# Gate product of an encoder layer: seven half-size block products per pair of token tiles instead of eight, all of h first

## The reference, cut to what matters

```python
mix = concatenate([o_att * silu(g_att), o_lru * silu(g_lru)])        # 512 + 512 channels
h = x + mix @ w_out                                                   # 1024 x 1024
e = (p @ w_ple) * sigmoid(h @ w_pg)                                   # w_ple 256 x 1024, w_pg 1024 x 1024
y = h + rms_norm(e, g_ple)
```

## Time and profile before

| | |
|---|---|
| device time, median of 3 runs | 1025.38 us (1024.9 to 1025.61) |
| span of the profiled execution, first to last instruction | 1022.9 us |
| PE busy | 1001.2 us, 98% |
| DVE, ACT, POOL busy | 657.0, 582.6, 496.6 us |
| matmuls | 5798 |
| granted TensorE clock | 0.999 of full speed |
| transfers | 150.34 MB, 147 GB/s on average |

### The profile page before, as it was taken

One profiled execution on the slowest core, in us unless ns is written; L12 is line 12 of the kernel. 1 busy time (PEld: TensorE's weight loads), 2 busy tenths in 40 slices (PEclk: granted clock), 3 DMA queues, 4 the chain that ended last, 5 costly groups with the idle time before them and its releaser, 6 DMA issues.

```text
span 1022.9 us, 15489 instructions
## 1 busy us (share of the span) xinstructions
PE 1001.2 (98%) x5798; PEld 798.6 (78%) x5798; DVE 657.0 (64%) x1062; ACT 582.6 (57%) x896; POOL 496.6 (49%) x400
## 2 busy tenths in 40 slices
PE   9999999999999999989999999999999999999997
PEld 7867777777788888878777777777788888888886
DVE  5645857592583350579999999999874454535423
ACT  7748485846641231569999999999942221112113
POOL 1163343626557440155676676666676334353421
PEclk9999999999999999999999999999999999999999
DMA  9751543323265527759876577433384223432321
GB/s 344 271 147 37 175 149 104 119 82 134 62 186 171 158 83 207 212 154 232 210 211 174 130 208 174 112 114 125 131 277 139 88 88 109 146 96 88 106 84 42
DMA packets 106329, 150.34 MB, mean 147 GB/s; under 512 B 10248, under 2 KB 69384, under 8 KB 106248
## 3 DMA queue, kind: packets, MB, share of 16 engines
q1 hardware_dynamic: 106112, 149.36, 48.6%
q10 hardware_dynamic: 144, 0.00, 0.0%
HBM read 102.07 MB, written 44.11 MB: 143 GB/s over the span
## 4 chain that ended last, share of the span: by engine, by line
PE 76%; DVE 14%; issue 7%; ACT 1%; POOL 1%; DMA 0%; DVEq 0%; SPq 0%; POOLq 0%; ACTq 0%
DVE E_ L1680 10%; PE b_ps L2008 6%; PE b_ps L2010 6%; PE b_ps L2009 6%; PE b_ps L1870 6%; PE b_ps L1872 5%; PE b_ps L1871 5%; PE g_ps L1872 4%; PE g_ps L1870 4%; PE g_ps L1871 4%; PE o_ps L2065 3%; PE s_ps L2021 3%; PE w_ps L1982 3%; PE h_ps L1870 2%; PE uT_ps L1945 2%
## 5 line engine op out<-in xcount | busy, mean ns | idle before, releaser
L1680 DVE CUSTOM_DVE_ANT_0 E_<-s_ps,bias 128x1024 f32<-128x1024 f32 (+1 forms) x184 | 188.2, 1057 | 10.0 <-PE s_ps L2021 9.8
L1266 ACT ACTIVATE E_<-E_,nmax 128x1024 f32<-128x1024 f32 (+1 forms) x184 | 186.6, 1018 | 13.3 <-DVE nmax L1680 13.3
L995 POOL TENSOR_TENSOR E_<-E_,ratio 128x576 f32<-128x576 f32 (+3 forms) x92 | 84.5, 919 | 92.7 <-DVE E_ L1696 92.7
L998 POOL TENSOR_TENSOR E_<-E_ 128x576 f32<-128x576 f32 (+3 forms) x92 | 103.6, 1126 | 7.2
L1872 PE MATMUL b_ps<-u_hi,wA_lo 128*128 128x512 f32 x256 | 99.8, 390 | 0.0
L2021 PE MATMUL s_ps<-KL,QL 128*128 128x512 f32 x256 | 88.8, 431 | 7.8 <-DVE nmax L1680 7.7
L1281 ACT ACTIVATE WT<-w_ps 128x1024 f32<-128x1024 f32 (+1 forms) x96 | 83.5, 869 | 4.2 <-PE w_ps L1982 3.8
L1982 PE MATMUL w_ps<-ident,E_ 128*128 128x128 f32 x624 | 83.5, 273 | 2.1 <-ACT WT L1281 2.0
L1870 PE MATMUL b_ps<-u_hi,wA_hi 128*128 128x512 f32 x216 | 85.5, 396 | 0.0
L1982 PEld LDWEIGHTS w_ps<-ident,E_ 128*128 128x128 f32 x624 | 72.6, 140 | 15.3 <-issue 6.3
L1871 PE MATMUL b_ps<-u_lo,wA_hi 128*128 128x512 f32 x216 | 84.1, 389 | 0.0
(11 more groups left out here) (265 smaller groups left out, 2420.3 us busy)
## 6 DMA issues: line engine op xcount, KB each, us to landing
QL<-qk_t SPq DMA_DIRECT2D x32, 256.0 KB, 7.3
KL<-qk_t SPq DMA_DIRECT2D x32, 256.0 KB, 8.5
bias<-line_d SPq DMA_DIRECT2D x8, 960.0 KB, 12.1
x_sb<-in_x SPq DMA_DIRECT2D x12, 512.0 KB, 9.0
z_ch<-z_stage SPq DMA_DIRECT2D x24, 256.0 KB, 2.9
qk_t<-qh SPq DMA_DIRECT2D x24, 256.0 KB, 2.3
qk_t<-ql SPq DMA_DIRECT2D x24, 256.0 KB, 2.8
mf<-mix_t SPq DMA_DIRECT2D x24, 256.0 KB, 4.0
```

What stands on the lines that cost most here:

```text
L998: gp.tensor_tensor(one, one, two, ALU.add).then_inc(w_gp, 1)
L1266: act.activation(e, e, ACT.Exp, bias=nmax[:, n % 5, c:c + 1], scale=-1.0, accum_out=sums[:, n % 5, c:c + 1]).then_inc(e_done, 1)
L1680: dve.tensor_tensor_reduce(weights_at(n)[:, c, 0:n_tok], s_ps[:, c, 0:n_tok], b[:, ::-1], -1.0, 3e38, ALU.add, ALU.min, nmax[:, n % 5, c:c ...
```

## The change

The gate product is computed for two token tiles at once, a left operand of 256 x 1,024 cut into four blocks of 128 x 512, A11, A12, A21, A22, against w_pg cut into four of 512 x 512. In place of the eight block products there are seven (Strassen's, in Winograd's form): S1 = A21 + A22, S2 = S1 - A11, S3 = A11 - A21, S4 = A12 - S2 on the left; on the right T1 = W12 - W11, T2 = W22 - T1, T3 = W22 - W12 (in W12's place), T4 = W21 - T2. Each product p1 to p7 is 12 matmuls (`gate_part`) into one of two banks, left_ps and right_ps. Three of the sums of products need a copy on ACT (`copy_sum`) and an addition on DVE (`joined`).

All of h comes first: a stage of its own runs turn_o and mix_product for tiles 1 to 11 and keeps h in four buffers, with tiles 0 to 7 also stored to a new DRAM tensor h_tok and loaded again later. Then six pairs follow, in the order of tiles 8/9, 10/11, 0/1, ... 6/7. The product of the pair's second tile takes part as r = 1, that of its first as r = 0. In the stage of h, from tile 2 on, o's squares are taken on ACT (`square_o`), its root is a reciprocal on DVE (`mean_square`) and a square root on ACT (`root_o`), and the scaling is eight small activations (`scale_o`) in place of one DVE operation. The splits and sums of the gate weights (`gate_weights` on DVE, `gate_high` on ACT, two on POOL) are operations on 2,048 elements, spread over the same stage. In the pairs, sums and splits of the turned h are made for the next pair while this one runs. The last pair is finished in halves of 512.

The sum of the counts: the gate product was 12 x 48 = 576 matmuls of 128x512 and is 6 x 7 x 12 = 504. Transposes of h stay 96, in fours.

```diff
+            def store_h(n):
+                sp.wait_ge(fin["h_done"], n + 1)
+                sp.dma_start(h_tok[n * P:(n + 1) * P, :], h_sb[:, n % 4, :]).then_inc(fin[f"h_out{n % 2}"], 16)
+            def load_h(g, r):
+                t, slot = tile_of(g, r), slot_of(g, r)
+                sp.wait_ge(fin["y_done"], 2 * (g - 2) + 2 - r)
+                sp.wait_ge(fin[f"h_out{t % 2}"], 16 * 4)
+                sp.dma_start(h_sb[:, slot, :], h_tok[t * P:(t + 1) * P, :]).then_inc(fin[f"h_in{r}"], 16)
...
-
-            def tail_io(n, s, i):
-
+            for n in range(NT):
                 if n + 3 < NT:
-                    load_o(n + 3, 1 - s)
+                    load_o(n + 3)
                 if n + 2 < NT:
                     load_mix(n + 2)
...
+                if 1 <= n < NT - 1:
+                    load_hp(n + 1)
+                    load_x_again(n + 1)
+                if 1 <= n <= NT - 4:
+                    store_h(n - 1)
+                if n in (1, 2):
+                    store_hp(IN_STEPS + 2 * n + 2)
+                    store_hp(IN_STEPS + 2 * n + 3)
...
+            for n in range(2, NT):
+                add_half(n)
+                if n == 8:
+                    gp.wait_ge(fin["w_sum"], 4)
+                    gp.wait_ge(fin["w_hi"], START["w_hi"] + 6)
+                    gp.tensor_tensor(wg_lo[:, BOTTOM, LEFT], wg_raw[:, BOTTOM, LEFT],
+                                     wg_hi[:, BOTTOM, LEFT].bitcast(F32), ALU.subtract).then_inc(fin["w_lo_gp"], 1)
+                if n == 10:
+                    gp.wait_ge(fin["w_hi"], START["w_hi"] + 7)
+                    gp.tensor_tensor(t4_lo[:], t4_raw[:], t4_hi[:].bitcast(F32), ALU.subtract
+                                     ).then_inc(fin["w_lo_gp"], 1)
...
+            def square_o(n):
+                act.wait_ge(fin[f"o_in{n % 2}"], 16 * (n // 2) + 16)
+                act.wait_ge(fin["o_red"], n)
+                act.activation(O_sq[:], o_in[n % 2][:], ACT.Square).then_inc(fin["o_sq"], 1)
+            def root_o(n):
+                act.wait_ge(fin["o_inv"], n - 1)
+                act.activation(rso[:, n % 2, :], rso[:, n % 2, :], ACT.Sqrt).then_inc(fin["o_rs"], 1)
+            def scale_o(n):
+                act.wait_ge(fin["o_rs"], n + 1)
+                act.wait_ge(fin["o_tr"], n)
+                for h in range(HEADS):
+                    c = slice(HV * h, HV * h + HV)
+                    scaled_o = act.activation(O_n[:, c], o_in[n % 2][:, c], ACT.Copy, scale=rso[:, n % 2, h:h + 1])
+                scaled_o.then_inc(fin["o_norm"], 1)
...
+            for n in range(NT):
+                if 1 <= n < NT - 1:
+                    mix_high(n + 1)
+                if n == 0:
+                    half_out(IN_STEPS + 3)
+                    gate_high(0)
+                if n in (1, 2):
+                    half_out(IN_STEPS + 2 * n + 2)
                 if n + 2 < NT:
...
+                    scale_o(n + 2)
+                if n in (1, 2):
+                    half_out(IN_STEPS + 2 * n + 3)
+                if n + 3 < NT:
+                    square_o(n + 3)
+                if n in (1, 2, 3, 4, 6, 7):
+                    gate_high({1: 1, 2: 2, 3: 3, 4: 4, 6: 5, 7: 6}[n])
+                if n + 3 < NT:
+                    root_o(n + 3)
+                if n == NT - 3:
+                    p_high(0, 1)
+                    p_high(0, 0)
...
+            def mean_square(n):
+                s = n % 2
+                dve.wait_ge(fin["o_sq"], n + 1)
+                dve.tensor_reduce(sso[:, s, :], O_sq[:].rearrange("p (a b) -> p a b", b=HV), AX.X, ALU.add
+                                  ).then_inc(fin["o_red"], 1)
+                dve.wait_ge(fin["o_red"], n + 1)
+                dve.tensor_scalar(mso[:, s, :], sso[:, s, :], 1.0 / HV, EPS, ALU.mult, ALU.add
+                                  ).then_inc(fin["o_ms"], 1)
+                dve.wait_ge(fin["o_ms"], n + 1)
+                dve.wait_ge(fin["o_norm"], n - 1)
+                dve.reciprocal(rso[:, s, :], mso[:, s, :]).then_inc(fin["o_inv"], 1)
...
+            def gate_weights(i):
+                if i == 0:
+                    dve.wait_ge(wg_in[0], 64)
+                    dve.wait_ge(o_mm, NSTEP // 2)
+                    minus(t1_raw[:], wg_raw[:, TOP, RIGHT], wg_raw[:, TOP, LEFT], fin["w_sum"])
+                if i == 1:
+                    dve.wait_ge(fin["w_hi"], START["w_hi"] + 1)
+                    dve.wait_ge(fin["w_sum"], 1)
+                    minus(wg_lo[:, TOP, LEFT], wg_raw[:, TOP, LEFT], wg_hi[:, TOP, LEFT].bitcast(F32), fin["w_lo"])
+                if i == 2:
+                    dve.wait_ge(wg_in[1], 64)
+                    minus(wg_raw[:, TOP, RIGHT], wg_raw[:, BOTTOM, RIGHT], wg_raw[:, TOP, RIGHT], fin["w_sum"])
...
+            mean_square(2)
+            for n in range(NT):
                 if n + 1 < NT:
-                    add_x(n + 1, 1 - s, i + s)
-                if n + 2 < NT:
-                    o_gate(n + 2)
+                    o_gate(n + 1)
+                if n:
+                    add_x(n - 1)
+                if n + 1 < NT:
+                    mix_low(n + 1)
                 if n + 3 < NT:
...
+                    mean_square(n + 3)
+                if n < 9:
+                    gate_weights(n)
...
+            def gate_part(dst, pair, high, low, start):
+                for k in range(LC):
+                    pe.matmul(dst, pair[0][:, k, :], high[:, k, :], start=start and k == 0, stop=False,
+                              skip_group_check=True)
+                    pe.matmul(dst, pair[0][:, k, :], low[:, k, :], start=False, stop=False, skip_group_check=True)
+                    mm = pe.matmul(dst, pair[1][:, k, :], high[:, k, :], start=False, stop=k == LC - 1,
+                                   skip_group_check=True)
+                mm.then_inc(fin["g_mm"], 1)
+            def p1(g):
+                pe.wait_ge(fin["t_dve"], 3 * g + 1)
+                if g:
+                    pe.wait_ge(fin["sig"], 4 * g - 1)
+                else:
+                    pe.wait_ge(fin["w_lo"], 1)
+                    pe.wait_ge(fin["h_done"], NT)
+                gate_part(left_ps[:], a11, wg_hi[:, TOP, LEFT], wg_lo[:, TOP, LEFT], True)
+            def p5(g):
+                pe.wait_ge(fin["s_lo"], 4 * g + 2)
+                if g:
+                    pe.wait_ge(fin["c_add"], START["c_add"] + 3 * g)
+                else:
+                    pe.wait_ge(fin["w_lo"], 2)
+                    pe.wait_ge(hp_done, 2 * NT)
+                gate_part(right_ps[:], s1, t1_hi, t1_lo, True)
...
+            for n in range(1, NT - 1):
+                turn_o(n + 1)
+                mix_product(n)
+                if n in (1, 2):
+                    half_tile(IN_STEPS + 2 * n + 2)
+                    half_tile(IN_STEPS + 2 * n + 3)
+            turn_a21(0)
+            turn_a11(0)
+            mix_product(NT - 1, lambda: turn_a22(0))
+            turn_a12(0)
+            for g in range(PAIRS):
+                p1(g)
+                p5(g)
+                p6(g)
+                embedding(g, 1)
+                if g < LAST:
+                    turn_a21(g + 1)
+                p7(g)
+                p3(g)
+                if g == LAST:
+                    embedding(g, 0)
+                    p2(g)
+                    p4(g)
+                    break
+                turn_a11(g + 1)
+                p4(g)
+                turn_a22(g + 1)
+                embedding(g, 0)
+                turn_a12(g + 1)
+                p2(g)
```

866 lines of the change are left out of this document (532 added, 334 removed).

## The result

Before 1025.49 us (median of 4 runs, 1024.9 to 1025.88), after **1044.74 us** (4 runs, 1043.88 to 1045.2): ratio **1.0187, interval [1.0173, 1.0202]**. The change makes the kernel 19.2 us slower, where 6.3 had been forecast, and the time lies 3.7 above the range. The profiled execution's span went from 1022.9 to 1043.1, +20.2.

A forecast was written before the change was run, and what follows sets the result against it. PE, busy 98% of the span, was taken to bound the kernel. -16.3 + 5.5 + 6.1 + 4.3 + 2.7 + 2.0 + 2.0 = +6.3 us, giving 1031.7 us, range 1019 to 1041.

The forecast's parts named there:

- The 16.3: Gate product on PE: 72 matmuls removed at 0.2267 us each, saving 16.3 us.
- the clock falls: Rival: PE's idle time at turn_o(2) lowers the clock, slowing later matmuls; +2.5 us, 1034.2 us; chance 0.20.
- the last rival: In the h stage x_rd's single buffer makes rounds of 9.3 against 6.05, costing 21 us: 1042.3 us; chance 0.12.
- (1) turn_o(2): First transposes of the h stage: PE waits for scale_o(2), queued on ScalarE behind half_out(19) and gate_high(0); +5.5 us.
- (2) VectorE's ring: In the h stage the VectorE and ScalarE round takes 6.9 us a tile against PE's 6.05; +6.1 us.
- (3) GpSimd's split: At iteration 8 of the h stage GpSimd's 2,048-element split holds VectorE's gate_weights(8), delaying PE's next tile; +4.3 us.
- (4) p1(0): Between h stage and gates, p1(0) waits for add_x(11), which waits for add_half(11) behind the t4 split; +2.7 us.
- Gate stage: In the pairs p5 waits for joined behind scaled_e, +1.1 in five pairs if GpSimd's s4 split goes first; taken +2.0 us.
- up to 3.3 more: Gate product: if the seven products ran at 0.233 a matmul, 3.3 us would be lost again; kept for the range.
- The end: After PE's last work the remaining operations and store take 8.0 us instead of some 6.0; +2.0 us.

The follow-up runs named there:

- Run 7: Changed kernel with PE's wait before turn_o(2) filled by 44 transposes of the identity matrix into an unread bank: 1042.16 us (one run).
- run 1: Changed kernel with a second x_rd buffer from tile 5 on: 1043.52 us, ratio 1.0188.
- run 17: Kernel of run 15 with a single x_rd buffer, as in the change: 1022.5 us.
- run 15: Kernel of run 12 with two weight blocks moved to the first pair, o's load one tile earlier, mf and p at 224 of 256 bytes: 1019.37 us.
- run 9: Kernel of run 8 with only 32 of 1,024 columns of x loaded for tiles 2 to 11 except 5: 1019.4 us.
- run 16: Kernel of run 15 with only 32 of 1,024 columns of x loaded for tiles 2 to 11 except 5: 1015.27 us.
- run 6: Changed kernel with VectorE's gate_weights ahead of mean_square in the h stage: 1041.31 us.
- run 3: Changed kernel with GpSimd's two 2,048-element splits moved from the h stage to the first pair of the gate stage: 1040.24 us.
- run 5: Changed kernel with joined(g,3) ahead of scaled_e(g,1) on VectorE and operands s1 to s3 moved by 32 bytes: 1043.03 us.
- run 2: Changed kernel with only 32 of 1,024 columns of x loaded for tiles 2 to 11: 1040.73 us.
- run 12: Kernel of run 11 with h's stores back where the change has them and wa, m, s1 to s3, p, mf at 96 of 128 bytes: 1020.67 us.
- run 11: Kernel of run 8 plus third o_in buffer, later h stores, GpSimd's sum with h between p's splits, operands 32 behind a multiple of 64: 1021.56 us.
- run 8: Changed kernel with all remedies: reordered ScalarE and VectorE work, two x_rd buffers, GpSimd splits and g_ple and p loads moved: 1023.18 us, ratio 0.9973.
- run 10: Kernel of run 8 with a third o_in buffer from tile 6 on: 1022.27 us, ratio 0.9974.

## Why the prediction was wrong

*Direction and frame: right.* The 16.3 came, and waits in the new h stage outweighed it. All terms but the 16.3 were forecast at +22.6 and measured at +36.5, so 13.9 were missing: 6.9 of clock, 4.0 of waits in the h stage, 2.7 in the gate stage and 0.3 at the end.

*The steps that failed.* The largest is the clock, which the sum put at nothing. The rival *the clock falls* was right for turn_o(2), 2.4 for its 2.5, but it was given 0.20, stood beside the forecast, and was looked for at one place. There were three falls in after, 6.9 in all. This was a plain omission: my own terms held a second wait of 4.3, and in the earlier trace rows I had read a fall after some 4 us of idleness. Run 7 shows the cause for the first of them.

The second step is in the last rival: "against it: the stage moves no more bytes a tile than before, and the shortest landing was 3.7". Bytes a tile had to be read against time a tile. The same 2 MB went into 20.5 us before (share 0.30, 99 GB/s) and into 7 to 8 after (0.84, 275 GB/s), and once in the stage 0.77 MB of g_ple and p came on top. A load lands behind what is issued with it: hp_sb, the store of h, o_in, Gt. The landing of 6.3 in the earlier trace rows was such a burst already; a mean share of 0.30 doesn't show it. The rival gave 1042.3 at a landing of 6.3, and was to decide from about 4.5 on; x_rd landed in 5.5 (median), 5.1 to 7.2 in the chain shown, and the time is 1044.7. It had 0.12. It was near in its time and not in its mechanism: a second buffer gained nothing to 1 (run 1) and 3 (run 17 against 15), the bytes 3 to 4 (runs 9 and 16), and the longest wait in the middle hung on o_in, not on x_rd.

*(1) turn_o(2): right.* 5.5 forecast, 5.7 measured. Its parts were a little off: eight small activations took 2.00, not 1.5, and gate_high(0) 1.90.

*(2) VectorE's ring: right in size, wrong as the bound.* 6.9 forecast, 7.07 in the first free tile (o_gate at 800.55 and 807.62), and run 6, which broke that ring, gained 3.4. But four of the six tiles after it came at 8.1 to 11.7. The term was 6.1, and the five waits of its tiles came to 10.1, 4.5 of them the one behind o_in.

*(3) GpSimd's split: right in size, wrong in the victim.* Forecast 4.3, by holding gate_weights(8); measured a wait of 5.6, of which 3.9 was the split and the rest the ring; run 3 gained 4.5. What it held was a TENSOR_SCALAR of eight elements. The prediction said "that one with at most one SBUF input doesn't contend; the trace agrees with both halves". The trace had shown that for readers of PSUM only. The Trainium skill (SBUF — State Buffer, "Who interferes with whom") says it only outside VectorE's two-port modes, and lists tensor_scalar among the operations that can enter them and then contend; that half I had not applied.

*(4) p1(0): wrong, small.* 2.7 forecast, 1.2 measured. Mix products came so late that add_half(11) was no longer behind them.

*Gate stage: the mechanism was right.* The prediction put scaled_e against GpSimd's split of s4, +1.1 a pair if the split goes first, and took 2.0 in all. It went first in all five pairs, at 0.66 each: 3.3. The reload of h fitted, as forecast, and was late by 0.28 only when run 5 delayed it. The "up to 3.3 more" for matmuls at 0.233 came as 1.4, in p5 to p7 alone.

*The end:* 2.0 forecast, 2.3 measured.

*Slips in the sums.* 0.35 + 5.68 is 6.03, not 6.05. Five iterations of 0.85 are 4.25, not 4.5. In (3) the block ends 10.4 - 6.9 = 3.5 late; 4.3 is its distance from PE's 6.05, and 0.85 of that could already stand in (2). The last rival's round is 9.2, not 9.3. Together they are about a microsecond in the forecast, and none decides the outcome.

## What to carry to other kernels

When a change gathers work of a long loop into a short stage, divide each tile's bytes by the tile's new time and put the result beside the highest rate of the trace, before looking at engines; a landing read in a quiet loop is the length of its burst and doesn't shrink when the bursts come closer. Then list what is queued on SyncE ahead of the load that is waited for, loads that belong to a later stage included. Put a price on the clock for each longer wait of PE: in these runs every wait of 2.4 or more in the stage was followed by a fall, and so were three of the four waits of 1.9 (runs 2, 5 and 12), but none of those of 2.0 to 2.25; each fall cost 1.5 to 2.7. Remedies for a chain of near-equal waits were worth 12 us one by one here and 21.6 together; two small edits came in with the rest, so how much of the surplus lies in their being together isn't shown.

## What the runs showed of the hardware

**Start addresses change the matmul's step.** In every group read here whose stationary and moving operands both start at 224 of 256 bytes the matmuls of 512 columns settle at a step of 0.227 (p1, p3, the embedding of after; all groups of run 15). In the other combinations read they step at 0.233: 192 with 224, either way round (p5, p6 and the mix product of even tiles of after; in the kernel before the mix product, which became fast as wa went from 192 to 224); 32 with 224 (embedding, run 11); 96 with 224 (embedding, run 12), though that is the same place of 128. Run 15 expected that the same place of 256 bytes is enough. That isn't shown, and the mix products of odd tiles of after speak against it: m_hi and wa both start at 192 there, in two of three matmuls, and the three still average 0.233. After transposes the first ten or so matmuls step unevenly at 0.224 to 0.236 in either case. Why this is so no run shows. It is worth 0.9 us to the kernel before (0.9991 [0.9982, 0.9999]), for two paddings of 32 and 96 bytes.

**VectorE and GpSimd hold each other in small operations too.** A TENSOR_SCALAR of 128x8 took 4.09 and 1.53 (after), 0.87 and 0.63 (run 8) beside a GpSimd operation on SBUF, and 0.17 alone, while the TENSOR_REDUCE just before it, with one SBUF input as well, kept its 0.69 (845 to 847 of after). GpSimd's addition took 4.1 to 4.5 beside a weight block of VectorE (runs 8 and 10) and 2.4 alone.
